# Normalising banded and memory attention through the gate instead of through the probabilities, with query layout on GpSimd

## The reference, cut to what matters

```
def banded_attention(q, k, v, max_dist, sink):
    ...
    p = jnp.exp(s - m[..., None])
    denom = jnp.sum(p, axis=-1)
    if sink is not None:
        denom = denom + jnp.exp(sink_b - m)
    o = jnp.einsum('nbhgqk,nbkhd->nbqhgd', p, vw.astype(jnp.float32))
    o = o / jnp.moveaxis(denom, -1, 2)[..., None]
...
        pc = jax.nn.softmax(sc, axis=-1)
        oc = jnp.einsum('bhsm,bmhd->bshd', pc, mv.astype(jnp.float32))
...
        y = jnp.concatenate([oa * jax.nn.silu(ga), ob * jax.nn.silu(gb),
                             oc * jax.nn.silu(gc)], axis=-1)
```

## Time and profile before

| what | value |
|---|---|
| median of 3 executions | 2164.6 us (2164.4 to 2168.8) |
| profiled execution | span 2163.3 us; the page gives no other time for it |
| PE busy | 2054.7 us, 95% of the span, 12892 matmuls |
| DVE busy | 1557.3 us, 72% |
| ACT busy | 1351.1 us, 62% |
| GpSimd busy | 114.9 us, 5% |

### The profile page before, as it was taken

How to read it: one execution, slowest core, us unless ns; L and a number is a source line. 1 busy time by engine, 2 the same in 40 slices (tenths; PEclk the granted TensorE clock), 3 DMA queues, 4 the chain that set the end, 5 groups by cost and what they waited for, 6 DMA issues and landing times. The chain is left out here.

```text
span 2163.3 us, 39340 instructions
## 1 busy us (share of the span) xinstructions
PE 2054.7 (95%) x12892; PEld 1717.7 (79%) x12892; DVE 1557.3 (72%) x4410; ACT 1351.1 (62%) x3520; POOL 114.9 (5%) x116
## 2 busy tenths in 40 slices
PE   5999899999999999999899999999899998999998
PEld 4787678888888888888777887888778887788886
DVE  6564674546664574446588989989799997888887
ACT  6454454544555464343699979989689998533333
POOL 1232310000000000002000000000000000000000
PEclk7999999999999999999799989989999999999999
DMA  4477576777577657589778676686869996245543
GB/s 157 144 243 217 170 240 179 221 242 218 154 225 223 219 182 244 199 276 273 179 147 157 133 142 135 131 166 121 166 149 214 232 270 179 98 158 175 174 158 113
DMA packets 351737, 401.40 MB, mean 186 GB/s; under 512 B 105617, under 2 KB 255249, under 8 KB 346689
## 3 DMA queue, kind: packets, MB, share of 16 engines
q1 hardware_dynamic: 343120, 364.80, 61.5%
q0 software_dynamic: 8432, 34.30, 5.1%
HBM read 255.62 MB, written 143.39 MB: 184 GB/s over the span
## 5 line engine op out<-in xcount | busy, mean ns | idle before, releaser
L854 PE MATMUL p_ps<-p_u_hi,p_w_hi 128*128 128x512 f32 x1344 | 534.7, 398 | 25.8 <-DVE p_p_c L739 10.6
L856 PE MATMUL p_ps<-p_u_hi,p_w_lo 128*128 128x512 f32 x1344 | 526.8, 392 | 0.0
L855 PE MATMUL p_ps<-p_u_lo,p_w_hi 128*128 128x512 f32 x1344 | 526.2, 392 | 0.0
L570 DVE TENSOR_TENSOR p_w_lo<-p_w_raw,p_w_hi 128x512 fp32r<-128x512 f32 x336 | 245.7, 732 | 331.4 <-ACT p_w_hi L423 329.8
L1621 ACT ACTIVATE probs<-probs,a_stat 128x256 f32<-128x256 f32 (+1 forms) x896 | 433.7, 489 | 49.2 <-DVE a_stat L1455 45.8
L423 ACT ACTIVATE p_w_hi<-p_w_raw 128x512 fp32r<-128x512 f32 x336 | 210.7, 628 | 331.7 <-PE p_ps L856 303.7
L854 PEld LDWEIGHTS p_ps<-p_u_hi,p_w_hi 128*128 128x128 f32 x1344 | 254.1, 189 | 86.1 <-DVE p_u_lo L577 12.0
L856 PEld LDWEIGHTS p_ps<-p_u_hi,p_w_lo 128*128 128x128 f32 x1344 | 254.0, 189 | 54.5
L1455 DVE CUSTOM_DVE_ANT_0 probs<-a_ps_s,fixed 128x256 f32<-128x256 f32 (+1 forms) x704 | 251.6, 396 | 63.2 <-PE a_ps_s L1354 61.9
L855 PEld LDWEIGHTS p_ps<-p_u_lo,p_w_hi 128*128 128x128 f32 x1344 | 254.4, 189 | 50.7
L1408 PE MATMUL a_ps_o<-a_pT,a_v 128*64 128x128 f32 x3320 | 256.7, 285 | 22.8 <-ACT a_pT L1645 21.5
(11 more groups left out here) (202 smaller groups left out, 2756.5 us busy)
## 6 DMA issues: line engine op xcount, KB each, us to landing
p_w_raw<-in_w_in SPq DMA_DIRECT2D x156, 256.0 KB, 3.6
p_w_raw<-scratch_w_s SPq DMA_DIRECT2D x144, 256.0 KB, 3.7
scratch_qk_hi<-p_out_a SPq DMA_DIRECT2D x80, 256.0 KB, 4.1
scratch_qk_lo<-p_out_b SPq DMA_DIRECT2D x80, 256.0 KB, 4.2
a_v<-scratch_v SPq DMA_DIRECT2D x40, 512.0 KB, 7.6
scratch_gate<-p_out_a SPq DMA_DIRECT2D x64, 256.0 KB, 3.9
scratch_v<-p_out_a SPq DMA_DIRECT2D x256, 64.0 KB, 2.3
a_gate<-scratch_gate SPq DMA_DIRECT2D x64, 256.0 KB, 5.9
```

The source lines that it names most:

```text
L570: nc.vector.tensor_tensor(w_lo[:, m % 3, :, :], w_raw[:, entry(j, g), :, :], w_hi[:, m % 3, :, :].bitcast(F32), ALU.subtract).then_inc(w_l ...
L854: nc.tensor.matmul(bank, hi, u_hi[j][:, k, :], start=j < 2 and k == 0, stop=False, skip_group_check=True)
L855: nc.tensor.matmul(bank, hi, u_lo[j][:, k, :], start=False, stop=False, skip_group_check=True)
L856: last = nc.tensor.matmul(bank, lo, u_hi[j][:, k, :], start=False, stop=k == KH - 1, skip_group_check=True)
```

## The change

For A and C, `scale` is gone. The value products take the exponentials as they are. PE instead runs `widen`: for each of a phase's 2 banks, eight float32 matmuls whose weights are one column of `coef` repeated 64 times and whose moving side is the identity, so that `ps_x` holds the reciprocals in the layout of the bank. DVE runs `scale_gate`, gate times `ps_x`, and `finish_bank` then multiplies the bank by that gate. As `ps_x` is the fourth place of `ps_s`, NS becomes 3 for A and C. `turn` waits for the exponentials (`sums_ready`) rather than for scaled probabilities. A's queries are laid out by GpSimd alone, one 128x2048 cast per phase. B keeps its order. The cut diff:

```diff
-    COPIES = {"B": 4, "A": 4, "C": 0}[kind]
-    NS = 3 if kind == "B" else 4
+    COPIES = {"B": 4, "A": 1, "C": 0}[kind]
+    NS = 3
...
+    def natural_copies(pool):
+
+        for p in range(2 * heads):
+            pool.wait_ge(q_loaded, 32 * p + 32)
+            if p < 2:
+                pool.wait_ge(prev.scores_ready, prev.TOTAL)
+            else:
+                pool.wait_ge(scores_ready, (p - 1) * NP)
+            nc.gpsimd.tensor_copy(q[:, 1 + p % 2, :].rearrange("p (b r a) -> p b r a", r=16, a=8),
+                                  q[:, 0, :].rearrange("p (r b a) -> p b r a", r=16, a=8).bitcast(F32)).then_inc(q_copied, 1)
...
             if prev and isinstance(h, int) and h + s == 0 and slot < NS:
-                if slot < prev.NS:
-                    pe.wait_ge(prev.max_ready, prev.TOTAL - prev.NS + 1 + slot)
-                if slot == 3 and prev.kind == "B":
-                    pe.wait_ge(prev.coef_ready, prev.phases)
+                pe.wait_ge(prev.max_ready, prev.TOTAL - prev.NS + 1 + slot)
...
-            pe.wait_ge(weighted, p * NP + e + 1)
+            pe.wait_ge(weighted if kind == "B" else sums_ready, p * NP + e + 1)
...
+        def widen(phase, e):
+
+            if kind == "B" or e % 4 != 1:
+                return
+            p, s, c = number(phase), phase[1], e // 4
+            n = p * NC + c
+            pe.wait_ge(coef_ready, p + 1 + (kind == "A"))
+            if n:
+                pe.wait_ge(gate_scaled, n)
+            elif prev.kind == "B":
+                pe.wait_ge(prev.coef_ready, prev.phases)
+            else:
+                pe.wait_ge(prev.gate_scaled, prev.phases * NC)
+            for i in range(4):
+                for j in range(2):
+                    u = FLAT[s][2 * (4 * c + i) + j]
+                    last = nc.tensor.matmul(place_of(ps_x[j * HD:(j + 1) * HD, :], u), coef[:, s, u.column:u.column + 1].broadcast_to([P, HD]),
+                                            ident[:], start=i == 0, stop=i == 3, skip_group_check=True)
+            last.then_inc(widened, 1)
...
         def scale(phase, e):
+            if kind != "B":
+                return
...
-            if kind == "A":
-                copy_natural(dve, phase, slot, lambda p, g: nc.vector.tensor_copy(
-                    *natural_part(p, 2 + g)).then_inc(q_copied, 1))
...
+        def scale_gate(phase, e):
+
+            if kind == "B" or e % 4 != 2:
+                return
+            h, s = phase
+            n = number(phase) * NC + e // 4
+            dve.wait_ge(widened, n + 1)
+            dve.wait_ge(gate_loaded[s], 32 * h + 32)
+            of, by = views(ps_x, s, e // 4)
+            nc.vector.tensor_tensor(by, of, by, ALU.mult).then_inc(gate_scaled, 1)
...
             else:
+                dve.wait_ge(gate_scaled, n + 1)
+                bank, by = views(ps_o[:, (MERGED + c) % 2, :], s, c)
                 nc.vector.tensor_tensor(by, bank, by, ALU.mult).then_inc(bank_read, 1)
...
-            if kind == "A":
-                copy_natural(act, phase, slot, lambda p, g: nc.scalar.activation(
-                    *natural_part(p, g), ACT.Copy).then_inc(q_copied, 1))
...
                     for x, e in (slot.two_before, slot.before):
                         x.parts.times_values(x.phase, e)
+                    x.parts.widen(x.phase, e)
...
+                if slot.before:
+                    x, e = slot.before
+                    x.parts.scale_gate(x.phase, e)
                 if slot.two_before:
                     x, e = slot.two_before
                     x.parts.finish(x.phase, e)
...
+                A.natural_copies(pool)
                 for n in range(4):
                     pool.wait_ge(A.done_sem, (9 + n) * NC)
                     load_sum(n)
```

More of the change, by code:

```diff
@@ L1159, in head_group @@
     scores_ready, max_ready, sums_ready = sem("scores_ready"), sem("max_ready"), sem("sums_ready")
-    weighted, turned, turned_copied = sem("weighted"), sem("turned"), sem("turned_copied")
+    weighted = sem("weighted") if kind == "B" else None
+    turned, turned_copied = sem("turned"), sem("turned_copied")
     values_done = sem("values_done")
@@ L1163, in head_group @@
     coef_ready = sem("coef_ready")
-    step, exps_ready = sem("step"), sem("exps_ready")
+    widened, gate_scaled = (sem("widened"), sem("gate_scaled")) if kind != "B" else (None, None)
+    step, exps_ready = (sem("step"), sem("exps_ready")) if kind != "C" else (None, None)
     if kind == "B":
@@ L1302, in natural_piece @@
                 by_residue(q[:, 0, :])[:, :, 32 * g:32 * g + 32].rearrange("p r (b a) -> p b r a", a=8))
-    def natural_part(p, g):
-        return (q[:, 1 + p % 2, g * CHUNK:(g + 1) * CHUNK].rearrange("p (b r a) -> p b r a", r=16, a=8),
-                by_residue(q[:, 0, :])[:, :, 32 * g:32 * g + 32].rearrange("p r (b a) -> p b r a", a=8).bitcast(F32))
     def tensor_parts(pe):
@@ L1350, in scores @@
                 u = FLAT[s][2 * slot + j]
-                out = ps_s[:, slot % NS, j, 2 * P - u.keys:]
+                out = ps_s[:, n % NS, j, 2 * P - u.keys:]
                 w = queries_of(q, u, {"B": None, "A": s, "C": number(phase) % 3}[kind])
@@ L1426, in turn @@
             last.then_inc(turned, 1)
-        return named(scores=scores, exchange=exchange, turn=turn, times_values=times_values)
+        def widen(phase, e):
[16 more added lines that the diff above has]
+            last.then_inc(widened, 1)
+        return named(scores=scores, exchange=exchange, turn=turn, widen=widen, times_values=times_values)
     def vector_parts(dve):
@@ L1432, in vector_parts @@
             dve.wait_ge(coef_ready, 1)
-        C1 = 1 if kind == "A" else 0
         def scores(phase, slot):
@@ L1455, in scores @@
                 last = nc.vector.tensor_tensor_reduce(
-                    out=probs[:, s, 2 * slot + j, a:], in0=ps_s[:, slot % NS, j, a:], in1=masks[u.kind][:, a:],
+                    out=probs[:, s, 2 * slot + j, a:], in0=ps_s[:, n % NS, j, a:], in1=masks[u.kind][:, a:],
                     scale=-SCALE, scalar=start, op0=ALU.add, op1=ALU.min,
@@ L1539, in scale @@
             if e == 0:
-                dve.wait_ge(coef_ready, p + 1 + C1)
+                dve.wait_ge(coef_ready, p + 1)
             for j in range(2):
@@ L1578, in add_far, with views @@
             return last
+        def views(bank, s, c):
+            if kind == "C":
+                return bank, gate[:, s, c * CHUNK:(c + 1) * CHUNK]
+            by = gate[:, s, :].rearrange("p (r a) -> p r a", a=HD)[:, :, 32 * c:32 * c + 32]
+            return bank.rearrange("p (u r a) -> p u r a", u=4, a=32), by.rearrange("p (u r) a -> p u r a", u=4)
+        def scale_gate(phase, e):
[7 more added lines that the diff above has]
+            nc.vector.tensor_tensor(by, of, by, ALU.mult).then_inc(gate_scaled, 1)
         def finish_bank(phase, d, c):
@@ L1609, in gated @@
             nc.vector.tensor_tensor(by, summed.rearrange("p u (r a) -> p u r a", a=32), by, ALU.mult).then_inc(y_ready, 1)
-        return named(scores=scores, exchange=exchange if kind == "B" else inverse, scale=scale, finish=finish, finish_rest=finish_rest, gated=gated, copy_queries=copy_queries)
+        return named(scores=scores, exchange=exchange if kind == "B" else inverse, scale=scale, scale_gate=scale_gate, finish=finish, finish_rest=finish_rest, gated=gated, copy_queries=copy_queries)
     def scalar_parts(act):
@@ L1678, in head_group @@
         kind=kind, heads=heads, phases=2 * heads, NP=NP, NS=NS, TAIL=TAIL, EARLY=EARLY, TOTAL=TOTAL,
-        scores_ready=scores_ready, values_done=values_done, max_ready=max_ready, turned=turned,
+        gate_scaled=gate_scaled, scores_ready=scores_ready, values_done=values_done, max_ready=max_ready, turned=turned,
         turned_copied=turned_copied, bank_read=bank_read, coef_ready=coef_ready, done_sem=done_sem, y_stored=y_stored,
-        q_copied=q_copied, copied_by=copied_by, natural_copied=natural_copied,
+        natural_copies=natural_copies, q_copied=q_copied, copied_by=copied_by, natural_copied=natural_copied,
         loads=loads, tensor_parts=tensor_parts, vector_parts=vector_parts, scalar_parts=scalar_parts)
```

## The result

The change makes the kernel slower: 2192.6 us (median of 4, 2189.8 to 2198.1) against 2164.5 us (median of 4), ratio 1.013, 95% interval 1.011 to 1.015. The forecast was 2186.0 us, range 2172 to 2200.

What follows compares the result with a forecast made beforehand. PE was taken to bound C outright and to have 1.1 us of slack per A round. Terms of +0.4, +6.7, +13.6, +2.6 and -1.8 gave +21.5 us on 2164.6, so 2186.1 us, range 2172 to 2200.

Steps and rivals of the forecast that it cites:

- What bounds: A and C rounds: PE bounds C outright; in A it has some 1.1 us slack per round, lost through DVE and ACT.
- my floor of 12.45: A rounds before the change: PE's own work is about 12.45 us of a 13.57 us round.
- Widen, 0.88 us per group: PE in A and C: 40 groups of eight widen matmuls, each group 16 records at 0.055 us.
- The row of the twins: PE's value products, same type, size and order as widen: 16 records for eight matmuls, used to price a group at 0.88 us.
- The prices of 1.44 us and of 0.44 us: Widen group rivals: column halves not overlapping, 1.44 us, 2208.5 us, 8%; one record per matmul, 0.44 us, 2168.6 us, 5%.
- The sum over A and C, +21.5 us: A and C rounds together: widen's groups less PE's slack and the dropped wait make the kernel 21.5 us slower.
- The wait for B's coefficients: A's first round, slot 3: with three score places PE no longer waits for B's coefficients, credited 1.8 us.
- Scaling removed, gain nothing by itself: DVE in A and C: loses 4.85 us per round, which brings nothing beyond PE's slack.
- Three places, cost 0: Scores in A and C: waiting for the maxima of slot n-3 instead of n-4 costs 0.
- The gate two slots sooner, cost 0: Gate product on DVE: the gate is needed two slots sooner, its reload arrives with some 5 us to spare, cost 0.
- Query copies moved, cost 0: A's query layout moved from DVE and ACT to GpSimd: 2.4 us per round, hidden even at several times the price, cost 0.
- The faster rival: A and C: PE's stream does not set the rounds, so removing scaling shortens them by 13.7 us, 2150.9 us; 4%.

Runs made afterwards that it cites:

- widen_a: The changed kernel with group C scaling its probabilities on DVE again, widen left in A alone: 2176.4 us, ratio 1.005 to the kernel before.
- widen_twice: The changed kernel with each group of eight widen matmuls issued twice: 2220.0 us, ratio 1.026 to the kernel before.
- gpsimd_only: The kernel before with GpSimd's layout of A's queries as its only change, scaling still on DVE: 2171.9 us, ratio 1.003.
- widen_only: The changed kernel with A's queries copied by DVE and ACT in four pieces again: 2182.7 us, ratio 1.010 to the kernel before.
- ns3: The kernel before with three places for A's and C's scores instead of four, nothing else changed: 2162.7 us, ratio 0.999.

## Why the prediction was right, and where it was off

- **What bounds.** C is pure PE work: shown by widen_a (12.18 us without widen) and by widen_twice (+1.76 for two more groups). A had slack on PE, lost in the loop through DVE and ACT: gpsimd_only has rounds of 12.69 and 12.72 us in which no cast runs, against 13.57 before. PE is busy for 12.0 and 12.1 us in them and DVE for 12.5, so they are not PE's floor. The A rounds with widen, in which PE has no gap, give 14.27 - 1.76 = 12.51 us, and my floor of 12.45 was 0.06 too low.
- **Widen, 0.88 us per group.** Exact, in the changed kernel and in widen_twice. The row of the twins was the right one; the record count (16 for eight) told more than the shape did. I called the eight value products "four pairs' worth"; they are two pairs' (two units each, two halves of the keys). The prices of 1.44 us and of 0.44 us fall. My 1.44 was itself low: the trace has the transposes' records 0.109 us apart, as my 0.09 counted up to a score that began 0.03 us behind the last of them, and 16 at 0.109 are 1.74 us. By the four passes that the Trainium skill states ("FP8 and Floating Point Precision", section "TensorE Precision Notes") and 128 columns at 2.4 GHz, the estimate was 1.7 us per group; the trace shows half of that, 0.88 us. Both fit together if the two column halves share the time. No run puts all eight matmuls into one half, so this sharing is argued and not shown.
- **The sum over A and C, +21.5 us.** widen_only gave +21.7 between A's start and the output projection, term by term: A's first phases -1.4 (forecast -1.4); the rounds of A's phases 2 to 11 and of C together +21.3 (forecast 20.3), of which A's nine rounds are +6.3, the way from A's phase 11 to C's first reciprocals +2.7 and C's seven measured rounds +12.3 (7 x 1.76); last round +1.8 (forecast +2.6). The sum came so close by luck in part, as the slips of +1.0 and -0.8 cancel: three groups lie in the last round and bring 0.6 us each, so PE alone did not set it. The wait for B's coefficients, 1.8 us at A's first scores, is gone as forecast. But ns3, which drops it too, gains only 0.5 us in A's first two phases and 1.2 in A to output, so the exact hit of -1.4 does not show that the wait was worth 1.8.
- **Scaling removed, gain nothing by itself.** Right. DVE fell to 8.4 us a round in C and nobody went faster.
- **Three places, cost 0.** Right, by ns3. **The gate two slots sooner, cost 0.** Right in the changed kernel, whose waits in C name no gate load.
- **Query copies moved, cost 0: wrong.** This is the step that failed, though the forecast as a whole held. I said the cast is hidden "even at several times the price", because nobody waits for GpSimd. I asked who waits for its result and not whom it holds up while it runs. Here it held up DVE's copy of the sink and, before that, two of B's scalings. In the profiled executions the layout on GpSimd cost +4.7 us in the changed kernel, 2.8 in A to output (329.5 against 326.7) and 1.9 in B's end (24.7 against 22.8), and left up to 10 us ungained in gpsimd_only (9 x (13.83 - 12.69)). I also took DVE's work in A after the change as 8.9 us; it was 9.7 in a normal round and 11.2 in the round with the blocked copy. The range held because the slip was small beside widen.
- **The rest of +29.1 us.** 24.5 lie in A to output and 2.6 in B's end. The remaining 2.1 us come before the first cast and are not explained by the change.
- **The faster rival** needed a group below 0.34 us. It was 0.88, so it falls as priced.

## What to carry to other kernels

Before work is moved from a busy engine to PE, look at the round in which PE is already full: there each microsecond added is a microsecond of the kernel, and the freed engine gives nothing back. Price a new matmul by its twin with the same type, shape and column halves, and count records, not program lines. For work moved to GpSimd, ask what DVE does meanwhile: a long GpSimd instruction can hold up a tiny DVE copy for nearly its whole length (1.70 of 1.90 us), and cutting it into pieces takes most of that back.

## What the runs showed that I had not expected

A GpSimd cast of 1.90 us holds DVE's SBUF-to-SBUF copies and scalings until it ends: 0.16 became 1.70 us for a copy of two columns, 0.61 became 2.11 for a pair of scalings, and 3.15 with the cast doubled. What takes one input from PSUM was not held. In the changed kernel 14 maxima of 128x256 and four products of gate and `ps_x` began while a cast ran, and they kept their 0.48 and 0.69 us. The Trainium skill, "SBUF — State Buffer", section "Who interferes with whom", says that the pair of ports shared by DVE and GpSimd is an exclusive lock held for a whole instruction, and that copies and `tensor_scalar` can take it. These runs agree: the held copies end 0.02 us after the cast, the held scalings 0.08 to 0.15. Applied to this kernel in the forecast, it would have put a wait of up to 1.9 us on DVE into each A round. The other way round GpSimd lost little: the 12 casts of gpsimd_only took 1.89 to 2.01 us each. In the forecast I had priced them at the 2.36 us of B's first phase. Splitting the cast into 16 raised GpSimd's own time from 1.91 to 4.2 us per phase (the records, 309 ns each, overlap) and still shortened the A round from 13.83 to 13.02 us.
